# Scan levels 0 to 6 of a gated recurrence: products with half the targets, two heads per bank

## What is computed

```python
# per head of 8: q, k, logf (T, 128), v (T, 128), f = exp(logf), k = 1 - f
# S_t = diag(f_t) S_{t-1} + k_t v_t^T,   o_t = S_t^T q_t
def step(S, inp):
    qb, kb, vb, gb = inp
    G = jnp.cumsum(gb, axis=-2)
    o_inter = jnp.einsum('bhtd,bhdv->bhtv', qb * jnp.exp(G), S)
    diff = G[:, :, :, None, :] - G[:, :, None, :, :]
    decay = jnp.exp(jnp.where(causal, diff, -jnp.inf))
    A = jnp.sum(qb[:, :, :, None, :] * kb[:, :, None, :, :] * decay, axis=-1)
    o = o_inter + jnp.einsum('bhts,bhsv->bhtv', A, vb)
```

## Time and profile before

| | us |
|---|---|
| median of 3 runs | 2410.13 |
| lowest, highest | 2409.72, 2411.78 |
| the profiled execution's own time | 2411.02 |
| its span in the trace | 2409.2 |

### The profile page before, as it was taken

How to read it: one execution, slowest core, us unless ns; L and a number is a source line. 1 busy time by engine, 2 the same in 40 slices (tenths; PEclk the granted TensorE clock), 3 DMA queues, 4 the chain that set the end, 5 groups by cost and what they waited for, 6 DMA issues and landing times.

```text
span 2409.2 us, 34143 instructions
## 1 busy us (share of the span) xinstructions
PE 2282.0 (95%) x13205; PEld 1981.3 (82%) x13205; DVE 830.2 (34%) x1290; ACT 780.1 (32%) x1109; POOL 929.0 (39%) x707
## 2 busy tenths in 40 slices
PE   6999999998798799999999899999988999999997
PEld 5888887786787578888787899999988689899886
DVE  4222103113455442222106422232149245555401
ACT  4333313122565544333314432212100323334311
POOL 3444444330202244444443444444434103544542
PEclk9999999997898999999999999999999869999999
DMA  4332322340000022323222222232210002232221
GB/s 148 97 95 87 105 87 88 96 142 18 1 2 1 1 79 89 102 88 104 87 87 88 70 87 87 88 101 90 84 40 1 18 1 88 88 100 91 90 102 61
DMA packets 150739, 179.51 MB, mean 75 GB/s; under 512 B 6926, under 2 KB 140399, under 8 KB 150655
## 3 DMA queue, kind: packets, MB, share of 16 engines
q1 hardware_dynamic: 150491, 178.35, 22.8%
q10 hardware_dynamic: 163, 0.04, 0.0%
HBM read 176.28 MB, written 2.10 MB: 74 GB/s over the span
## 4 chain that ended last, share of the span: by engine, by line
PE 61%; issue 20%; POOL 9%; DVE 7%; ACT 2%; SPq 1%; DMA 0%; POOLq 0%; DVEq 0%; ACTq 0%
PE ps L1505 38%; PE ps L1637 10%; POOL wlo L605 9%; PE ps L1942 2%; PE ps L1866 2%; PE ps L1836 2%; DVE Ad L1415 1%; PE ps L1848 1%; PE ps L1762 1%; DVE Q L1432 1%; PE ps L1751 1%; PE ps L1834 1%; DVE tmp L1014 0%; PE ps L1862 0%; PE ps L1831 0%
## 5 line engine op out<-in xcount | busy, mean ns | idle before, releaser
L605 POOL TENSOR_TENSOR wlo<-raw,whi 128x512 fp32r<-128x512 f32 x638 | 836.2, 1342 | 1153.2 <-ACT whi L674 1153.2
L1505 PE MATMUL ps<-xh,whi 128*128 128x512 f32 (+2 forms) x2432 | 699.1, 333 | 12.9 <-DVE gateT L1293 8.8
L1505 PE MATMUL ps<-xh,wlo 128*128 128x512 f32 (+2 forms) x2432 | 700.5, 334 | 0.0
L1505 PE MATMUL ps<-xl,whi 128*128 128x512 f32 (+2 forms) x2432 | 699.7, 334 | 0.0
L674 ACT ACTIVATE whi<-raw 128x2048 fp32r<-128x2048 f32 x160 | 304.8, 1905 | 757.2 <-PE ps L1505 447.3
L1505 PEld LDWEIGHTS ps<-xh,whi 128*128 128x128 f32 x2432 | 416.8, 190 | 62.2 <-DVE gateT L1293 7.8
L1505 PEld LDWEIGHTS ps<-xl,whi 128*128 128x128 f32 x2432 | 415.3, 190 | 45.5
L1505 PEld LDWEIGHTS ps<-xh,wlo 128*128 128x128 f32 x2432 | 413.9, 189 | 46.0
L1637 PE MATMUL ps<-act_l,whi 128*128 (+1 forms) x528 | 208.7, 395 | 0.0
L1637 PE MATMUL ps<-act_h,whi 128*128 (+1 forms) x528 | 208.7, 395 | 0.0
L1637 PE MATMUL ps<-act_h,wlo 128*128 (+1 forms) x528 | 208.7, 395 | 0.0
(11 more groups left out here) (305 smaller groups left out, 2671.6 us busy)
## 6 DMA issues: line engine op xcount, KB each, us to landing
raw<-in_w_in SPq DMA_DIRECT2D x47, 1024.0 KB, 5.0
raw<-in_ffn_wg SPq DMA_DIRECT2D x22, 1024.0 KB, 5.3
raw<-in_ffn_wu SPq DMA_DIRECT2D x22, 1024.0 KB, 5.3
raw<-in_ffn_wd SPq DMA_DIRECT2D x22, 1024.0 KB, 4.9
raw<-in_w_up SPq DMA_DIRECT2D x22, 1024.0 KB, 5.1
raw<-in_w_down SPq DMA_DIRECT2D x11, 1024.0 KB, 4.9
raw<-in_w_out SPq DMA_DIRECT2D x8, 1024.0 KB, 5.0
raw<-in_ple_w_gate SPq DMA_DIRECT2D x4, 1024.0 KB, 5.2
```

The lines of the kernel that those rows point to most:

```text
L605: last = nc.gpsimd.tensor_tensor(wlo[:, slot, d], raw[:, slot, d], whi[:, slot, d].bitcast(F32), ALU.subtract)
L1505: last = mm(ps[:, j * banks + b, 0:n], w[:, k, e * P:(e + 1) * P], x[:, k, c0:c0 + n], start=(k == 0 and q == 0), stop=(k == KD - 1 and q ...
```

## The change

At levels 0 to 6, only the targets of the second halves are multiplied: from each tile of 128 targets, the 64 whose position lies in the second half of its pair, in blocks of w. A product is then 128 sources by 64 targets. The results of two heads fill one bank (2 heads, 4 tiles, 64 targets: 512 columns), and one `copy_predicated` takes both over, into every second block of `Ad`, with every second block of the mask. So at each of these levels there are 4 entries of the sequence in place of 8, and a group waits for two selections in place of four. Level -1, the meta tokens, levels 7 and 8, the updates of Q, K and the decays, and their number stay as they are. The whole diff:

```diff
--- before.py
+++ after.py
@@ -122,11 +122,16 @@
     return used_count(first - 1) if first else 1
 
 
+def heads_of(lv):
+
+    return 2 if 0 <= lv < 7 else 1
+
+
 def level_sequence():
 
     seq, b = [], 0
     for lv in range(-1, LEVELS):
-        for n in range(VH):
+        for n in range(0, VH, heads_of(lv)):
             seq.append((lv, n, b % 7))
             b += 1
         if 1 << max(lv, 0) < M:
@@ -1411,7 +1416,13 @@
                     if lv < 7 and n == META:
                         nc.vector.copy_predicated(Am[:], levelmask[0:M, lv + 1, 0:M].unsqueeze(1).to_broadcast([M, VH, M]),
                                                   ps[0:M, bank, 0:VH * M].rearrange("p (n m) -> p n m", n=VH)).then_inc(lev_sel, 1)
-                    elif lv < 7:
+                    elif 0 <= lv < 7:
+                        w = 1 << lv
+                        nc.vector.copy_predicated(
+                            Ad[:, n:n + 2, :].rearrange("p n (i b e w) -> p (n i) b e w", i=TT, e=2, w=w)[:, :, :, 1, :],
+                            levelmask[:, lv + 1, :].rearrange("p (b e w) -> p b e w", e=2, w=w)[:, :, 1, :].unsqueeze(1).to_broadcast([P, 2 * TT, HD // w, w]),
+                            ps[:, bank, :].rearrange("p (q b w) -> p q b w", q=2 * TT, w=w)).then_inc(lev_sel, 1)
+                    elif lv < 0:
                         nc.vector.copy_predicated(Ad[:, n, :].rearrange("p (i t) -> p i t", i=TT),
                                                   levelmask[:, lv + 1, :].unsqueeze(1).to_broadcast([P, TT, P]),
                                                   ps[:, bank, :].rearrange("p (i t) -> p i t", i=TT)).then_inc(lev_sel, 1)
@@ -1424,7 +1435,7 @@
                 nb = S // (2 * H)
                 for g in range(2):
                     heads = slice(HG * g, HG * (g + 1))
-                    select(lv, HG * (g + 1) - 1)
+                    select(lv, HG * (g + 1) - heads_of(lv))
                     if lv < 0:
                         link(nc.vector.tensor_tensor(Q[:, heads, M:T], Q[:, heads, M:T], Fg[:, heads, M:T], ALU.mult))
                     else:
@@ -1960,7 +1971,14 @@
                 if n == META:
                     for m in range(VH):
                         last = mm(ps[0:M, bank, m * M:(m + 1) * M], K[:, m, 0:M], Q[:, m, 0:M], start=True, stop=True)
-                elif lv < 7:
+                elif 0 <= lv < 7:
+                    for m in range(2):
+                        for i in range(TT):
+                            c = m * 4 * HD + i * HD
+                            last = mm(ps[:, bank, c:c + HD].rearrange("p (b w) -> p b w", w=1 << lv), K[:, n + m, xc(i)],
+                                      pairs(Q[:, n + m:n + m + 1], M + i * P, M + (i + 1) * P, 1 << lv)[:, 0, :, 1, :],
+                                      start=True, stop=True)
+                elif lv < 0:
                     for i in range(TT):
                         last = mm(ps[:, bank, i * P:(i + 1) * P], K[:, n, xc(i)], Q[:, n, xc(i)], start=True, stop=True)
                 elif lv == 7:
```

## The result

| | before | after |
|---|---|---|
| median, us | 2410.38 (4 runs, 2409.72 to 2411.78) | 2434.74 (4 runs, 2432.14 to 2435.4) |
| profiled execution, own time | 2411.02 | 2434.57 |
| its span | 2409.2 | 2432.8 |
| PE busy | 2282.0 | 2314.4 |
| DVE busy | 830.2 | 827.5 |

The change makes the kernel slower: its median is 24.4 us higher, and the ratio of its runs to those of the kernel before is 1.0095 with a 95% interval of 1.0082 to 1.0107 (the quotient of the two medians alone is 1.0101). The scan stage, from the first product of level -1 to the start of the output, takes 122.6 us instead of 100.4: 22.2 us of it. The rest, seen in these two profiled executions, lies outside: the unchanged program ahead of the stage ended 3.0 us later, and what follows the stage was 1.6 us shorter (523.2 to the end of the span against 524.8).

What follows compares the result with a forecast made beforehand. VectorE bounds levels 0 to 6 before the change, TensorE at 1.2 GHz after it. Level 7's second group moves from 1870.6 to 1893.4, so 2411.0 + 22.8 = 2433.8, said as 2434; range 2424 to 2441.

Steps and rivals of the forecast that it cites:

- half-clock case: Levels 1 to 6: TensorE stays at 1.2 GHz, 13.66 us a level; the end moves by 22.8 us to 2434; chance 0.80.
- Selections, 28 x 0.62 = 17.4 us less on VectorE, and nothing for the stride: VectorE, levels 0 to 6: 56 selections become 28 at 0.62 us each, 17.4 us less, strided writes adding nothing.
- 64 records a level whatever the targets: 7.3 us at full clock, 13.66 at half: TensorE, levels 0 to 6: halved targets save nothing at full clock; at half clock a record comes every 0.2135 us.
- The gap ahead of level 1 stays, 3.9 us, and loses the clock: TensorE before level 1: GpSimd's key update delays the Q update, a 3.9 us gap remains, the clock falls to 1.2 GHz.
- Narrow products keep a clock but don't regain it: TensorE, levels 1 to 6: 64-column products behave like line 1762's 62-column ones, keeping full clock but not regaining it.
- VectorE and GpSimd hide behind TensorE: Half-clock groups last 6.8 us; the other group's VectorE and GpSimd work takes 5 us at most, 6 at level 1.
- Meta products 0.8 us a level at half clock: TensorE, levels 1 to 3: the meta tokens' 16 records count 0.8 us each level at half clock, 2.4 in all.
- Levels 1 to 6: 84.4 us; the second group of level 7 at 109.4 us after the first product of level -1: TensorE: 82.0 us for six levels plus 2.4 for meta products; level 7's second group starts at 1893.4 instead of 1870.6.
- The first: Clock returns at a level's gapless products; VectorE saves 17.4 us, GpSimd waits return 9: gain 8, 2403 (2396 to 2409); chance 0.08.
- The second: 64-column records keep 113 ns when the clock halves, 7.3 us a level at either clock: 2400; chance 0.04.
- The third: Strided selections take twice as long and the clock comes back: VectorE as loaded as before, 2411; chance 0.03.
- The fourth: Slow clock for only part of the levels; each full-clock level takes 6.1 us less: 2412 to 2427; chance 0.05.

Runs made afterwards that it cites:

- the fillers: The change plus 20 products of 384 columns that nobody reads, put where TensorE idles in levels 1 to 3 and 7: 2400.47 us.
- wide products with half selections: Against the kernel before: products keep 128 targets, one head per bank, VectorE makes 8 selections a level of second-half targets only, 256 elements each: 2408.57 us.
- wide fillers before level -1 and in the gaps: The change plus unread 384-column products where TensorE idles, 20 in levels 1 to 3 and 7, and 6 more before level -1: 2398.29 us.
- narrow fillers: The change plus unread 64-column products where TensorE idles, three in place of each 384-column one, same places: 2406.09 us.

## Why the prediction was right

**The half-clock case came in.** 2434 was predicted for the likeliest case, 2434.74 measured. The mechanism was the one forecast. That the number is off by less than 1 us is partly luck: the sum left out 3.0 and -1.6 us that lie outside the stage. Step by step, against the text:

- *Selections, 28 x 0.62 = 17.4 us less on VectorE, and nothing for the stride.* Wrong in size, without consequence. From level 2 on a selection takes 0.7 us (0.62 from start to start with the fillers), but at levels 0 and 1, where the blocks are one or two elements long, it takes 1.15. The row that I took it from, the Q update on every second element, does not hold for this instruction. Eight of the 28 selections cost 0.5 us more than said, so VectorE gains about 13 us of selections instead of 17. The bound of twice as long was the nearer one for two levels out of seven. At 1.2 GHz it all lay in VectorE's idle time.
- *64 records a level whatever the targets: 7.3 us at full clock, 13.66 at half.* Right. 7.55 us for level 0 and 7.26 with the clock held, 13.85 from the start of level 1 to its meta products, 13.67 a level at levels 4 to 6 (1851.35 to 1892.37). The row of another line, with 62 columns, carried this term.
- *The gap ahead of level 1 stays, 3.9 us, and loses the clock.* Right: 3.76 us, and 0.50 from 1807.4. But the way there was another: the 1.25 us that the first group's selections were to save came to 0.22 (2.31 us against 2.53), since they are those of level 0. The wait for GpSimd's key update stands as forecast: the Q update took 1.45 us instead of 1.23, and line 1449 at 1804.44 takes 3.70 us, as line 1438 did before. This wait would have covered the larger saving too, so the error on the selections left no trace in the gap.
- *Narrow products keep a clock but don't regain it.* Right, and shown by edits, see above.
- *VectorE and GpSimd hide behind TensorE.* Right: no gap on TensorE from level 1 into level 7. The Q updates were put at 1.2 us and took about 2.4; VectorE had the room.
- *Meta products 0.8 us a level at half clock.* Too high. Their row is 0.61 us against 0.57; 16 records in about 0.54. Three levels: 1.6 instead of 2.4. Levels 1 to 3 took 0.2 us each more than the 13.66 of the sum, which makes up most of that.
- *Levels 1 to 6: 84.4 us; the second group of level 7 at 109.4 us after the first product of level -1 (1893.4 - 1784.0).* Measured 84.2 (1808.19 to 1892.37) and, from the record starts, 109.2.
- *From there as before, 13.8 us.* 13.4.

The stage was said to grow by 22.8 us and grew by 22.2.

**The rivals.** The first (the clock comes back as before, 2403) did not happen for the changed kernel. The wide products with half selections did get the clock back behind their gaps: 2408.57, with runs from 2400 to 2412. The rival's working, 17.4 us less some 9 for waits on GpSimd, gave 8, and that stage came out 7.9 shorter, but this doesn't confirm the working: it is another kernel, with 8 small selections a level instead of 4 large ones, and its VectorE was to save about 11 us. The second, records that keep their length when the clock halves, fell: 0.2136 us a record with 64 columns at 1.2 GHz (41.02 / 192). There the Trainium skill's rule (TensorE: Matmul & The Clock Gate, "LDWEIGHTS (loading the stationary operand)"), 107 ns for 128 columns of weights, holds for 2.4 GHz and is half of what was measured at 1.2. The 2400 that the prediction gives for this case is the rival's, where VectorE bounds the levels; six levels of 6.8 us put into its sum would give 2393. The third fell with the clock: it needed selections of 1.3 us at every level, and only levels 0 and 1 came near. The fourth, a slow clock for only part of the levels, is what levels 4 to 6 alone did, and there the same program gave runs on both sides of the kernel before.

**The best kernel of the study** is the change with wide fillers before level -1 and in the gaps, 2398.29 us, 0.9940 of the kernel before (0.9927 to 0.9954). It computes the same. But a table of fillers is tuned to this order and these gaps. Wide products with half selections get 0.9972 with no filler.

## What to carry to other kernels

Before narrowing a product, look for what sets its pace: here it was not the targets. With 128 columns of weights each, 62, 64 and 128 targets all came at about 113 ns a record at 2.4 GHz, so half the targets gave TensorE nothing. And look at the clock in the stretch: where gaps already cost it, the products behind the gap must be such as brought it back before; in this kernel the wide ones did, and the narrow ones held 1.2 GHz for 88.7 us. To lighten the engine that reads the results, narrow its reads, not the products. And when one engine gets faster, look at what it releases sooner: full clock at level 1 brought a key update of GpSimd into VectorE's way and cost 3 us.

## What the runs showed of the hardware

- A `copy_predicated` of 512 elements per partition took 0.62 us from start to start with blocks of 4 and more elements, and 1.15 us with blocks of one or two (levels 0 and 1), with mask and target strided alike; of 256 elements, 0.44 us as a median record and 0.79 at most. A `tensor_tensor` on the same stride lost nothing (1.23 us against 1.20).
- Meta products of 16 by 16 columns hardly slowed at 1.2 GHz: 0.61 us for 16 records against 0.57, where records with 128 columns of weights went from 113 to 214 ns.
- Runs of 30 narrow fillers and 32 or more narrow products, with gaps of 0.2 to 0.4 us between them at levels 1 to 6, kept the 2.4 GHz that they began with: the clock was full from 1790.0 to 1895.6.
- Most gaps of over 3 us in the stage lost the clock, and one of 2.22 us did not the earlier trace rows. But length alone does not decide: in one and the same execution (wide products, half selections) a gap of 2.65 us lost it and one of 3.10 us did not, and a gap of 2.94 us ahead of level 8 of the changed kernel did not either. Where a slow stretch ended differed between executions of one program, and with it the next gap.
- VectorE's product of 128 by 64 elements took 2.10 us instead of 0.21 when it met a key update of GpSimd (1811.92 to 1815.16), and ended just behind it, at 1815.25; selections from PSUM beside such updates were not held up (706 to 762 ns for all 64 before the change).
- The program behind the stage took 520.0 to 525.0 us in the profiled executions, the same instructions in each, with TensorE's mean granted clock at 0.95 in the short ones and 0.94 in the long ones.
